# Four layers of a hybrid trunk on one core: the last MLP's fourth quarter as seven block products, with its column sums prepared two pieces ahead and its first two token tiles finished on ScalarE and GpSimd

## The reference

```python
def rms_norm(x, g, eps=NORM_EPS):
    xf = x.astype(jnp.float32)
    y = xf * lax.rsqrt(jnp.mean(xf * xf, axis=-1, keepdims=True) + eps)
    return (y * g.astype(jnp.float32)).astype(x.dtype)

def sq_relu_mlp(x, w_in, w_out):
    return jnp.square(jax.nn.relu(x @ w_in)) @ w_out
...
    for layer in range(DEPTH):
        ...
        h = h + rms_norm(m, norm_mix_post[layer])
        f = sq_relu_mlp(rms_norm(h, norm_ffn_pre[layer]), ffn_w_in[layer], ffn_w_out[layer])
        h = h + rms_norm(f, norm_ffn_post[layer])
    return h
```

## Time and profile before

| what | us |
|---|---|
| runs shown: median of 3 (lowest to highest) | 1475.97 (1475.69 to 1479.87) |
| the profiled execution, its own time | 1476.38 |
| its span | 1474.6 |
| TensorE busy in it | 1434.8 (97%) |
| VectorE, ScalarE, GpSimd busy | 921.6, 538.2, 87.1 |
| mean granted TensorE clock | 0.986 of full |

### The profile page before, as it was taken

The page is one execution under the profiler, slowest core; times in us unless marked ns, Lnnn a source line. Parts: engine busy times, 40 slices in busy tenths (PEclk is TensorE's granted clock), DMA queues, the critical chain, the costliest instruction groups (busy, mean ns, idle before and its releaser), DMA issues.

```text
span 1474.6 us, 22076 instructions
## 1 busy us (share of the span) xinstructions
PE 1434.8 (97%) x9650; PEld 1181.9 (80%) x9650; DVE 921.6 (63%) x1200; ACT 538.2 (36%) x632; POOL 87.1 (6%) x89
## 2 busy tenths in 40 slices
PE   9999999998999999998999999999998999999997
PEld 6778787777888888887888888888887788888786
DVE  7768676667655565654756445355447876868754
ACT  7555454533312222223343332332434433433322
POOL 0000000012010100001200000000003000000000
PEclk9999999998999999999999999999998999999999
DMA  5211111101474654731222122222130352434332
GB/s 187 73 36 59 50 59 45 59 30 42 178 266 143 224 181 175 263 112 60 86 68 100 62 86 92 81 86 86 62 110 29 132 182 86 171 115 166 134 110 62
DMA packets 30623, 160.21 MB, mean 109 GB/s; under 512 B 2816, under 2 KB 6912, under 8 KB 15552
## 3 DMA queue, kind: packets, MB, share of 16 engines
q1 hardware_dynamic: 23456, 130.73, 25.0%
q0 software_dynamic: 7072, 28.08, 5.4%
HBM read 144.12 MB, written 14.68 MB: 108 GB/s over the span
## 4 chain that ended last, share of the span: by engine, by line
PE 89%; DVE 6%; ACT 2%; issue 1%; DMA 1%; POOL 0%; DVEq 0%; POOLq 0%
PE bank L388 21%; PE bank L394 20%; PE bank L391 20%; PE bank L691 2%; PE bank L695 2%; PE bank L694 2%; PE bank L1681 2%; PE bank L1675 2%; PE bank L1678 2%; PE bank L993 2%; PE bank L402 1%; DMA raw<-weights 1%; PE bank L1000 1%; DVE WL L346 1%; PE bank L593 1%
## 5 line engine op out<-in xcount | busy, mean ns | idle before, releaser
L388 PE MATMUL bank<-XH,WH 128*128 128x512 f32 x944 | 379.4, 402 | 15.4 <-DVE XL L481 12.6
L391 PE MATMUL bank<-XL,WH 128*128 128x512 f32 x944 | 371.2, 393 | 0.0
L394 PE MATMUL bank<-XH,WL 128*128 128x512 f32 x944 | 371.0, 393 | 0.0
L346 DVE TENSOR_TENSOR WL<-raw,WH 128x2048 fp32r<-128x2048 f32 (+1 forms) x99 | 222.1, 2245 | 136.7 <-ACT WH L340 136.6
L340 ACT ACTIVATE WH<-raw 128x2048 fp32r<-128x2048 f32 (+1 forms) x99 | 185.2, 1872 | 189.9 <-DMA raw<-weights 189.8
L388 PEld LDWEIGHTS bank<-XH,WH 128*128 128x128 f32 x944 | 179.5, 190 | 58.8 <-issue 19.5
L394 PEld LDWEIGHTS bank<-XH,WL 128*128 128x128 f32 x944 | 179.4, 190 | 38.7
L391 PEld LDWEIGHTS bank<-XL,WH 128*128 128x128 f32 x944 | 179.7, 190 | 38.2 <-issue 2.1
L845 ACT ACTIVATE AH<-relu 128x512 fp32r<-128x512 f32 (+1 forms) x64 | 37.9, 592 | 216.4 <-DVE relu L873 216.4
L388 PE MATMUL bank<-AH,WH 128*128 128x512 f32 x256 | 99.7, 390 | 0.0
L391 PE MATMUL bank<-AL,WH 128*128 128x512 f32 x256 | 99.6, 389 | 0.0
(11 more groups left out here) (360 smaller groups left out, 2339.3 us busy)
## 6 DMA issues: line engine op xcount, KB each, us to landing
raw<-weights SPq DMA_DIRECT2D x104, 1024.0 KB, 4.8
block<-weights POOLq DMA_DIRECT2D x12, 1024.0 KB, 7.6
sums_of_blocks<-block POOLq DMA_DIRECT2D x12, 1024.0 KB, 5.3
raw<-sums_of_blocks SPq DMA_DIRECT2D x12, 1024.0 KB, 4.8
raw<-weights SPq DMA_DIRECT2D x8, 512.0 KB, 4.5
h<-x_fm SPq DMA_DIRECT2D x4, 512.0 KB, 8.1
out_tm<-h SPq DMA_DIRECT2D x8, 256.0 KB, 2.6
rc<-ret_const POOLq DMA_DIRECT2D x1, 1536.0 KB, 8.1
```

Source lines behind the costliest of these rows:

```text
L346: nc.vector.tensor_tensor(WL[i][:, :n], raw[i][:, :n], WH[i][:, :n], ALU.subtract).then_inc(S("w_lo"), 1)
L388: mm = pe.matmul(bank[b][:], wh, xh, start=(k == 0), stop=False)
L391: mm = pe.matmul(bank[b][:], wh, xl, start=False, stop=False)
L394: mm = pe.matmul(bank[b][:], wl, xh, start=False, stop=(k == len(xs) - 1))
```

## The change

`SEVEN` becomes 4, so the fourth quarter of the last MLP is done by seven block products too: 168 matmuls instead of 192, and 7 chunks in place of 4. `out_by_token_*` go. Four more pieces of weight sums (16 in all) are made in the first MLP, at every odd j from j = 5 of quarter 0 to j = 3 of quarter 2, and GpSimd loads piece n + 2 right after piece n is stored, starting when two `AL` tiles are there. The closing norm is cut into helpers (`out_square`, `out_root`, `out_term`, `out_sum`, `out_inverse`, `out_stored`). Token tiles 0 and 1 are complete after P5; for them ScalarE scales the terms (`scale_terms`) and GpSimd adds them to `h` (`first_outputs`) while P6 runs; tiles 2 and 3 end on VectorE as before. `uT` moves to the memory of `XH` and `XL`. The gain row's load waits for `sums_lo` of the fourth quarter.

```diff
-SEVEN = 3
+SEVEN = QUARTERS
...
+                if q < QUARTERS - 1:
+                    continue
+                for t, b in enumerate(banks):
+                    if i in (1, 5):
+                        act.wait_ge(S(f"acc_free{b}"), now[t])
+                        out_square(act, t, i // 5)
+                    if i == 6:
+                        act.wait_ge(S("first_final"), t + 1)
+                        out_square(act, 2 + t, 0)
+                        act.wait_ge(S(f"acc_free{b}"), now[t])
+                        out_square(act, 2 + t, 1)
+                        out_root(act, 2 + t)
+                if i == 5:
+                    for t in range(2):
+                        out_root(act, t)
+                    for t in range(2):
+                        scale_terms(act, t)
...
+        def first_outputs(pool):
+            pool.wait_ge(S("h_by_token"), 2 * TT)
+            for t in range(2):
+                for n in range(2):
+                    pool.wait_ge(S("term_scaled"), 2 * t + n + 1)
+                    u, at = term_and_place(t, n)
+                    nc.gpsimd.tensor_tensor(at, u, at, ALU.add).then_inc(S("first_outputs"), 1)
+
+        def scale_terms(act, t):
+            act.wait_ge(S("token_rstd"), t + 1)
+            for n in range(2):
+                act.wait_ge(S("token_term"), OUT_ORDER.index((t, n)) + 1)
+                u = out_part(uT, t, n)
+                nc.scalar.activation(u, u, ACT.Copy, scale=post_rstd[:, t:t + 1]).then_inc(S("term_scaled"), 1)
...
+                    if q == QUARTERS - 1 and i in (3, 5):
+                        last = added[0, i // 5, t]
+                        dve.wait_ge(S(f"acc_free{last[0]}"), last[1])
+                        out_term(dve, t, i // 5)
+                    if q == QUARTERS - 1 and i == 6:
+                        dve.wait_ge(S("first_final"), t + 1)
+                        out_term(dve, 2 + t, 0)
+                        dve.wait_ge(S(f"acc_free{b}"), u)
+                        out_term(dve, 2 + t, 1)
+                        out_sum(dve, 2 + t)
+                if q == QUARTERS - 1 and i >= 5:
+                    for t in range(2):
+                        if i == 5:
+                            out_sum(dve, t)
+                    for t in range(2):
+                        out_inverse(dve, 2 * (i - 5) + t)
+                        if i == 6:
+                            out_stored(dve, 2 + t)
...
+            pool.wait_ge(S("a_lo"), 2)
+            load(0)
+            load(1)
             for n, (q, cols) in enumerate(pieces):
-
-
-
-                pool.wait_ge(S("a_lo"), 8 * (n // 4) + 4 + n % 4)
-                load(n)
                 pool.wait_ge(S("sum_step"), 4 * n + 4)
                 pool.dma_start(sums_of_blocks[q, :, :, cols].rearrange("k p c -> p k c"), block[n % 2][:]
                                ).then_inc(S("sums_stored"), 16)
+                if n + 2 < len(pieces):
+                    load(n + 2)
...
-                    if not layer and q < SEVEN and j in (9, 11, 13, 15):
-                        weight_sums_dve(dve, 4 * q + j // 2 - 4)
+                    if not layer and j % 2 and 0 <= 8 * q + j // 2 - 2 < SEVEN * PIECES:
+                        weight_sums_dve(dve, 8 * q + j // 2 - 2)
```

More of the change, by code:

```diff
@@ L571, in turn_h_act @@
                 nc.scalar.activation(to, bank[4 + 2 * (t % 2) + n].rearrange("p (k c) -> p k c", c=P), ACT.Copy).then_inc(S("h_by_token"), 1)
-        def out_by_token_pe(pe, use, c, done):
-            for n, banks in enumerate(TOKEN_BANKS):
-                for b in banks:
-                    u = use.next(b)
-                    if u > 1:
-                        pe.wait_ge(S(f"acc_free{b}"), u - 1)
-                for half in range(2):
-                    cj = c + 4 + 2 * n + half
-                    chunk_ready(pe, cj)
-                    for t, b in enumerate(banks):
-                        tok = slice(t * P, (t + 1) * P)
-                        for k in range(4):
-                            kt = 4 * half + k
-                            if n == 0 and t == 0:
-                                pe.wait_ge(S("a_lo"), done + kt + 1)
-                            wh, wl = (w[cj % RING][:, k * T:(k + 1) * T] for w in (WH, WL))
-                            mm = pe.matmul(bank[b][:], AH[:, kt, tok], wh, start=(kt == 0), stop=False)
-                            if t == 0 and k == 0:
-                                mm.then_inc(S("chunk_left"), 1)
-                            pe.matmul(bank[b][:], AH[:, kt, tok], wl, start=False, stop=False)
-                            mm = pe.matmul(bank[b][:], AL[:, kt, tok], wh, start=False, stop=(kt == KT - 1))
-                        if half == 1:
-                            mm.then_inc(S(f"acc_full{b}"), 1)
@@ L700, in seven_act @@
                 split_halves_hi(act, c + 6 + i, 7 * q + i)
-                for b in banks:
-                    use.next(b)
+                now = [use.next(b) for b in banks]
                 if i == 0:
                     sums_high(act, q, 3)
+                if q < QUARTERS - 1:
[10 more added lines that the diff above has]
+                        out_root(act, 2 + t)
@@ new lines, in out_sum, with out_inverse, term_and_place @@
+        def out_sum(dve, t):
+            dve.wait_ge(S("token_squares"), OUT_ORDER.index((t, 1)) + 1)
+            nc.vector.tensor_tensor(squares[:, 2, t:t + 1], squares[:, 0, t:t + 1], squares[:, 1, t:t + 1],
+                                    ALU.add).then_inc(S("token_sum"), 1)
+        def out_inverse(dve, t):
+            dve.wait_ge(S("token_root"), t + 1)
+            nc.vector.reciprocal(post_rstd[:, t:t + 1], post_root[:, t:t + 1]).then_inc(S("token_rstd"), 1)
+        def term_and_place(t, n):
+            return out_part(uT, t, n).rearrange("p (k c) -> p k c", c=P), hT[t][:, 4 * n:4 * n + 4, :]
@@ L839, in ffn_act @@
                     b = j % 4
-                    if layer and q < SEVEN and j > 4:
+                    if layer and j > 4:
                         sums_high(act, q, j - 5)
@@ L853, in ffn_act @@
                         turn_h_act(act, j)
[L854 removed]
+                if layer:
                     seven_act(act, use, c, q)
[L856 to L857 removed]
             if not layer:
```

124 lines of the change are left out of this document (46 added, 78 removed).

## The result

| | before | changed |
|---|---|---|
| median, 5 runs each | 1476.54 us (1475.69 to 1479.87) | 1486.74 us (1479.86 to 1488.83) |
| ratio, 95% interval | | 1.0058 [1.0039, 1.0077] |
| the profiled execution | 1476.38 us, span 1474.6 | 1479.86 us, span 1478.1 |
| mean granted TensorE clock | 0.986 | 0.982 |

The changed kernel is slower by 0.6%, and the median lies 6.8 us above the forecast of 1479.9 and outside its range. Two things have to be explained apart. The profiled execution of the changed kernel is the quickest of its five; it took the time that was forecast. The other four took 1484.4 to 1488.8. What they do is not in this first profile; a profile of another execution of the same kernel, under the experiments, shows it. (With two more executions the median before is 1476.54 us, where the forecast started from 1475.97.)

What follows compares the result with a forecast made beforehand. TensorE's matmul count and pauses, then VectorE's tail, were taken to bound the kernel. Terms -5.4 + 0 + 2.9 + 2.1 + 2.8 + 1.6, +3.9 with last digits kept, on 1475.97 gave 1479.9 us; range 1474.8 to 1482.8.

Steps and rivals of the forecast that it cites:

- step 4: First MLP, quarter 0: piece 0 delays `AL` of j = 7, so TensorE pauses, +2.8 us; elsewhere pieces fit, blocks in time.
- the first rival: First MLP, quarter 0: the pieces' loads also hold up a weight chunk, giving 1481.3 to 1482.7 us; chance 0.15.
- step 5: First MLP, behind the 2.8 us pause: the granted clock falls to 1.2 GHz for a while, +1.6 us, bounds 0 and 3.2.
- Steps 1 and 2: Last MLP: 24 fewer matmuls in the fourth quarter, -5.4 us; the pause before P5 moves there from quarter 2, 0 us.
- Step 3: End of last MLP: VectorE's tail grows +2.9 us by token tiles' work and +2.1 us by GpSimd's additions holding up VectorE.

Runs made afterwards that it cites:

- the execution of 1488.35 us: The changed kernel, unaltered, run again and profiled in a slow execution; that rerun's median of 8 was 1486.79 us, ratio 1.0054.
- the pieces alone: The kernel before with only its twelve pieces of weight sums moved to the new places and loaded two ahead: 1487.38 us, ratio 1.0063.
- the last MLP alone: The changed last MLP on the first MLP of the kernel before, its fourth quarter reading the third quarter's sums: 1475.29 us, ratio 0.9984.
- the first profile from j = 9 on: The changed kernel with every piece two odd tiles later, starting at j = 9 of quarter 0: profiled execution 1473.84 us, median 1474.41 us, ratio 0.9978.

## Why the prediction was wrong, and what in it was right

**The mechanism of step 4 was right and half of it was missed.** The pause near 392 us came at the forecast place and size (2.84 us for 2.8), for the forecast reason: `AL` of j = 7 behind piece 0. Putting each piece one odd tile later removes it. What was missed is in quarters 1 and 2.

**What failed is the sentence in step 4 that blocks come in time:** "a store and a load, some 14 us, against 19 us until the buffer's next turn". The 14 us were a store of some 5 and a load of some 8, each as it lands in the profile of before. There GpSimd issues the store first and the other buffer's load 0.76 us behind it:

```profile
402.18 0.76 POOL L773 DMA_DIRECT2D sums_of_blocks<-block  x1 [24.17 <-DVE block L786]
402.94 0.75 POOL L764 DMA_DIRECT2D block<-weights  x1
```

The new order turns them round: the load waits for a landed store, by then the next piece is done, and its store goes out 0.75 us behind the load. The load's 8 us held (7.0, median in the execution of 1488.35); the store's 5 did not (10.5), and it is the term that was mis-sized. GpSimd's order of waits adds 1.3 us, from 481.86 to 483.20, to the turn followed above. A turn of 23.1 us against 21.8 was measured in the place of 14 + 2.8. That brings pauses of 2.7 and 1.3 us and one more fall of the clock in quarters 1 and 2, which the forecast said would not be. It is the first rival's idea (too many megabytes at once) at another time: in quarters 1 and 2 and not in quarter 0, with the store held up most, and a chunk's load too (10.0 us at 460.54).

The evidence: the pieces alone bring it (ratio 1.0063), the last MLP alone does not (0.9984); with half of each load, and nothing else changed, it is gone (1.0022); with the pieces one or two odd tiles later, and so a first store that lands before its turn is over, it does not begin (0.9976, 0.9978). None of these runs parts the store's place behind the load from the bytes in flight. A run with loads two ahead and stores on a queue of their own would, and was not made. What makes one execution of the changed kernel leave the long turns after six pieces and another not is open: no run was made for it.

**The fall of the clock (step 5):** 7 matmuls, 1.6 us, as forecast. After the pause of 2.7 us in quarter 1 the mean granted clock over 5 us was 0.66 again. But the step's reason, that a pause longer than one that brought a fall brings one too, did not hold: behind the pause of 2.9 us in the half-load run the clock was 1.00, as it was behind that of 2.0 us before P5 in the execution of 1488.35 us, and in the first profile from j = 9 on it was 0.66 behind a start only 0.86 us after the one before it, at 356.03. So the 1.6 us came in the changed kernel's two profiles, and not by a rule of the pause's length. A mean of 0.66 is a mix of the two levels, 1.2 and 2.4 GHz. The Trainium skill ("TensorE: Matmul & The Clock Gate", "What's actually happening") has the clock fall only after a wholly idle stretch, which read strictly would have spared these pauses; the rows with a fall say otherwise, here as in the earlier trace rows, and that of the half-load run does not.

**Steps 1 and 2:** -5.4 us, right: 168 matmuls. The pause before P5 did move from quarter 2 to the fourth, and a load of 512 KB beside P5's chunk is its cause, but it is 0.8 us there (1454.30 to 1455.30 between two starts) in place of 1.4. Its size goes with that chunk's landing: 0.8 us for 7.0, 1.4 for 7.6, 2.0 for 8.3 in the execution of 1488.35 us.

**Step 3 was sized too high, in both terms:** 8.3 us of tail for 10.0. Without GpSimd the tail is 7.1, so the token tiles' own work costs 2.1 (forecast 2.9), and the additions 1.2 (forecast 2.1) in that pair of profiles. They do hold VectorE up as foreseen, even more (2.9 us, three of its instructions, one of them 0.15 us long); what was missed is that VectorE has a wait of 1.3 us for ScalarE's square in the same stretch, which takes up more than a third of it. The Trainium skill ("SBUF — State Buffer", "Who interferes with whom") says that a VectorE operation with two SBUF inputs and a GpSimd operation that reads SBUF exclude each other, and that the one that starts first keeps the other waiting for its whole length. The rows agree for two inputs of 128x1 (1.21 us in place of 0.15) as for 128x512, and an addition with one input in PSUM was left alone.

**Summed by what was measured:** -5.4 - 0.6 + 3.3 + 2.84 + 1.6 = +1.7 for an execution without the long turns. That the profiled one took +3.5, close to the forecast's 3.9, is partly luck: 2.1 us of it stood ahead of the first MLP, and two terms that were too high make up for it.

## What to carry to other kernels

A transfer's time to landing, taken from a profile, holds for its place in the queue and the company in which it ran. Where a change turns round a load and a store that go out together on one queue, the turn must be summed with their new times, and with the queue's own order of waits. Against the turn that the consumers allow it should keep room: 3.7 us held here, turns of 1.6 with one of 0.5 among them held in the one execution profiled, and none gave a kernel that takes 1479 in one execution and 1488 in the next. And where executions of a kernel lie apart by more than those of its neighbour, the profile of the quickest says little about the median; a profile of a slow one is needed.

## What the runs showed that was not expected

- What the same 1 MB store takes depends on what stands ahead of it. With a load 0.75 us behind it on GpSimd's queue it landed in 5.3 us in the kernel before (median; 5.3 to 6.2), and in the run with the store first in 5.3 to 6.9, even with a chunk's load issued less than 2 us behind. With a chunk's load in the same moment it took 9.0 (389.47), and with the load 0.75 us ahead of it on GpSimd's queue and a chunk's load within a microsecond 10.3 to 11.0 (in the execution of 1488.35 us). The Trainium skill ("DMA: Bandwidth & Descriptors", "Queues, rings and completion order") has each DMA engine take turns between the queues that have work. By that the load at the head of GpSimd's queue and the chunk's load on SyncE's would share the engines, and the store behind the first would come last. In the stretch from 470 us they landed at 478.96, 480.00 and 482.18, which agrees, but no run here puts the store on a queue of its own to show it.
- A loop with two buffers can run in two ways: with stores of 5 to 6 us and room, or with stores of 10 us and none. The quick execution shows both, with the change from one to the other at 450 us.
- Moving the gain row's load 10 us ahead only moved its harm: 6.8 us for the chunk beside it, and a pause of the same size one product sooner, before P4. With a chunk's load about every 5.5 us (1434, 1440, 1445) neither of the two places tried was free for half a megabyte.
